# Expert selection and gate scatter of a PEER layer: two steps of one token tile, or four groups of one token tile and four heads

## The chip, the cores and the metric

The kernel runs on one core of one Trainium2 chip. The time is the device time of one execution in microseconds (us), and the figure compared is the median over runs. Engines are called PE (TensorE matmul), PEld (its weight loads), DVE (VectorE), ACT (ScalarE), POOL (GpSimd) and SP (SyncE, which issues the plain DMAs).

## What is computed

Two transformer blocks in float32 on 256 tokens of width 2048. The first is a hybrid mixer with a gated FFN, the second a mixer of two attention branches followed by a PEER layer. The change touches only the PEER layer (`peer_ffn` of the reference, here for one block of 128 tokens):

```python
q = einsum('td,dhk->thk', xb, w_q).reshape(128, 8, 2, 64)        # 8 heads, two halves
s = einsum('thpc,hpnc->thpn', q, sub_keys)                       # 128 keys per half
s1, i1 = top_k(s[:, :, 0], 16);  s2, i2 = top_k(s[:, :, 1], 16)
cand_s = s1[..., :, None] + s2[..., None, :]                     # 256 candidates per head
cand_i = i1[..., :, None] * 128 + i2[..., None, :]
top_s, pos = top_k(cand_s, 16);  expert = take_along_axis(cand_i, pos)
g = softmax(top_s)
a = gelu(einsum('thkd,td->thk', u_emb[expert], xb))
out = einsum('thk,thkd->td', g * a, v_emb[expert])
```

There are 16384 experts. Then the residual and a last RMS norm follow.

## The kernel before

**Dense experts.** The kernel gathers no rows of the two expert tables. It computes gelu(U x) for all 16384 experts, multiplies by a gate matrix that is zero where an expert was not chosen, and multiplies by V. The gate matrix is `table` in HBM (16384 experts x 256 tokens, float32), zeroed long before (32 DMAs from SP that landed in the first block's FFN). GpSimd fills it: `put(q, head)` (line 2649) issues 16 indirect DMAs of 128 elements each, which add the softmax weights `wts[q]` of one token tile q (128 tokens) and one head at the places `eidx[q]`. Each of these is one "put" below, so there are 2 x 8 x 16 = 256. The adds of different heads of one tile may hit the same element, so `put` first waits until all puts of that tile's earlier heads have landed (`g.wait_ge(d_put[q], 16 * 16 * head)`).

**Chunks and slots.** All weights stream through the core in chunks of up to 128 x 1024 float32 (512 KB), in the order `PLAN`. SP loads chunk i into one of four buffers `raw` once DVE has finished with chunk i - 4. A float32 product is made of three fp32r products of high and low parts: ACT copies the high part into one of three buffers `wh` (`cut`, line 2168), DVE subtracts it to get the low part `wl` (`cut`, line 1424), and PE runs three matmuls per 128 x 128 tile (lines 918 to 920). ACT may write `wh` of chunk i when PE is through with chunk i - 3. A slot is one chunk counted from the first U chunk, U0. U takes slots 0 to 255 (two chunks per tile of 128 experts, 24 matmuls of 256 columns each), V with its first 1024 columns takes slots 256 to 383 (12 matmuls of 512 columns each), V with its other columns comes last. In slot i, ACT and DVE cut chunk i + 2, so a cut has some two slots before PE needs it.

**High parts in PSUM.** From slot 46 to the start of V (`in_psum`, line 209), ACT makes a second copy of the high part in a PSUM buffer `ph` (line 2180; two buffers, the older must have been read), and DVE subtracts that one in place of `wh`.

**Selection.** In a written-out order, `_sides3` (line 87) hands each step of the selection to a slot. Each step has an estimated cost on DVE, a slot takes off 1.5 us of what is owed, and not more than 2.7 us may be owed. For each tile q: `top` for 8 heads (the 16 best of 128 in each half, two parts), `cand` for 4 pairs of heads (sums and the 16 best of 256, two parts), `soft` (softmax: the exponential runs on ACT between two parts of DVE), `place` (the two index halves are picked out of 16 by comparing with an iota, multiplying head by head and summing; three parts for each half) and `index` (the place in `table`, released to GpSimd by `idx_ok`). DVE works them off in its slot loop, after `read_u` (line 2094; every second slot, reads one U tile out of PSUM) and before the slot's cut. By this order tile 0 has its index in slot 48 and tile 1 in slot 96. GpSimd then issues five heads of tile 0; after the second index three times a head of tile 1 and one of tile 0; and then five heads of tile 1.

**Into V.** SP waits (line 885) until all 256 puts have landed before it loads the first gate tile `gt` (128 x 256 of `table`), and behind that load in its queue stand the V chunks. `times_gate` (DVE, line 2101) multiplies gelu by the gate two slots before PE needs the tile, `coef_high` and `coef_low` split the product. `cand` waits (`d_spill`) for a DMA that saves the tokens `x2t`, whose place it takes.

Of the kernel before, what the change touches and what calls it, by code (L numbers as in the profile page):

```python
# [12 lines left out]
ALU = mybir.AluOpType  # L13
# [72 lines left out]

def _sides3():
    at = [[] for _ in range(3 * 128 + 8)]
    work = []
    for q in range(2):  # L90
        for i in range(8):
            work += [("top", (q, i, 0), 1.95), ("top", (q, i, 1), 1.35)]
        for i in range(4):
            work += [("cand", (q, i, 0), 3.5), ("cand", (q, i, 1), 1.9)]
        work += [("soft", (q, 0), 0.3), ("soft", (q, 1), 0.9)]
        for i in range(2):
            work += [("place", (q, i, 0), 2.6), ("place", (q, i, 1), 2.3), ("place", (q, i, 2), 2.2)]
        work += [("index", q, 0.4)]
# [5 lines left out]
    for name, a, us in work:  # L104
# [5 lines left out]
        if name == "soft" and a[1] == 1 and slot == last["soft"]:  # L110
# [99 lines left out]

def in_psum(i):

    return U0 + 46 <= i < AT["V", 0, 0]
# [264 lines left out]
def build(nc, A, out):  # L478
# [179 lines left out]
    gsum = carve(8)  # L658

# [761 lines left out]
    def _(v):  # L1421
# [598 lines left out]
        def cand_3(q, i, part):  # L2020
# [5 lines left out]
            if i == 0:  # L2026
                v.wait_ge(d_spill, 16)
                v.tensor_copy(f16[:, q, :, :], x16[:, q, :, :]).then_inc(own.up(), 1)
# [6 lines left out]
        def soft_3(q, part):  # L2035
            gw = sel[:, 2, :].rearrange("p (h s) -> p h s", h=8)
            if part == 0:
                after(own.n)
                v.tensor_tensor(gw, tv[:, q, :, :], tv[:, q, :, 0:1].to_broadcast([128, 8, 16]),
                                ALU.subtract).then_inc(soft_v, 1)  # L2040
                return
            v.wait_ge(soft_a, q + 1)
            v.tensor_reduce(gsum, gw, AX.X, ALU.add).then_inc(own.up(), 1)
            after(own.n)
            v.reciprocal(gsum, gsum).then_inc(own.up(), 1)
            after(own.n)
            v.tensor_tensor(wts[q].rearrange("p (h s) -> p h s", h=8), gw, gsum.unsqueeze(2).to_broadcast([128, 8, 16]),
                            ALU.mult).then_inc(own.up(), 1)

        def place_3(q, i, part):  # L2050

            xs = f16[:, q, :, :].rearrange("p (h two) k -> p h two k", two=2)[:, :, i, :]
            after(own.n)
            if part == 0:
                if i == 0:
                    pv = tp[:, q, :, :].rearrange("p h s -> p (h s)")
                    v.tensor_scalar(tpi[:, 0, :], pv, 4, None, ALU.logical_shift_right).then_inc(own.up(), 1)
                    v.tensor_scalar(tpi[:, 1, :], pv, 15, None, ALU.bitwise_and).then_inc(own.up(), 1)
                    for n in range(2):
                        after(own.n - 1)  # L2060
                        v.tensor_copy(kf[:, n, :], tpi[:, n, :]).then_inc(own.up(), 1)
# [724 lines left out]
```

## Time and profile before

| | us |
|---|---|
| runs | 3227.93, 3237.88, 3237.24 |
| median | 3237.24 |
| the profiled execution | 3235.74 |
| its span, first to last instruction | 3233.9 |
| PE busy in it | 3190.6 (99%) |
| DVE busy | 2095.7 (65%) |
| ACT busy | 1778.7 (55%) |
| POOL busy | 458.2 (14%) |
| mean granted TensorE clock | 0.995 |

The profile is of one execution. Times in it are counted from the start of its span. The part concerned lies between 1780 us, where U begins, and 2510 us, where V has begun. Busy time of PE includes waiting inside the pipeline and overlaps, so a wait of PE is read from the view of waits and not from the share. "Issue" as what ended an idle time means that nothing which the profile shows released the engine.

### The profile page before, as it was taken

The page shows a single profiled execution, that of the slowest core. Times are in us where ns is not written, and L with a number is a line of the kernel's source. Part 1 is how long each engine was busy: PE and PEld are TensorE (multiplying, and loading weights), DVE is VectorE, ACT ScalarE, POOL GpSimd, SP SyncE. Part 2 cuts the span into 40 slices and gives each one's busy share as a digit, 9 for nine tenths or more (in the row PEclk, how much of TensorE's full clock was granted, in tenths as well). Part 3 has the DMA queues.
Part 4 walks back from the last instruction along what each step waited for, and adds up shares of the span by engine and source line. Part 5 has one row for each costly group of instructions (what it writes and reads, how often), then busy time and mean ns, then how long its engine had stood idle before and what let it go on. Part 6 is the DMA issues. An engine that isn't in the chain of part 4 may idle for free.

```text
span 3233.9 us, 58767 instructions
## 1 busy us (share of the span) xinstructions
PE 3190.6 (99%) x24234; PEld 3030.5 (94%) x24234; DVE 2095.7 (65%) x3347; ACT 1778.7 (55%) x2546; POOL 458.2 (14%) x320
## 2 busy tenths in 40 slices
PE   9999999999999999999999999999996999999998
PEld 9999999999999999999999999999996888888887
DVE  7987486666664487665665898655553666665655
ACT  5556454444444455544554468777774444444544
POOL 0000200000000100000000026677666000000000
PEclk9999999999999999999999999999998999999999
DMA  6443556666666656444555567777775777766554
GB/s 219 153 145 140 177 195 231 230 226 224 222 189 198 193 168 209 145 158 169 191 195 201 197 191 188 196 195 194 194 194 128 239 234 234 236 220 208 188 188 163
DMA packets 228698, 627.77 MB, mean 194 GB/s; under 512 B 59248, under 2 KB 77776, under 8 KB 228304
## 3 DMA queue, kind: packets, MB, share of 16 engines
q1 hardware_dynamic: 191568, 623.87, 57.8%
q0 software_dynamic: 36864, 0.15, 3.2%
q8 instruction: 192, 3.15, 0.4%
q14 instruction: 74, 0.61, 0.1%
HBM read 601.27 MB, written 21.10 MB: 192 GB/s over the span
## 4 chain that ended last, share of the span: by engine, by line
PE 79%; POOL 12%; issue 5%; DMA 2%; DVE 1%; ACT 1%; SPq 0%; POOLq 0%; DVEq 0%; ACTq 0%
PE ps L919 25%; PE ps L918 25%; PE ps L920 25%; POOL table L2654 12%; DMA table<-w_loose 1%; PE ps L973 0%; DVE wl L1430 0%; PE ps L925 0%; PE ps L945 0%; PE ps L1168 0%; DMA raw<-in_in1k 0%; ACT wh L2175 0%; PE ps L1191 0%; PE ps L1188 0%; PE ps L1360 0%
## 5 line engine op out<-in xcount | busy, mean ns | idle before, releaser
L2175 ACT CAST wh<-raw 128x1024 fp32r<-128x1024 f32 (+2 forms) x1118 | 1161.3, 1039 | 1111.5 <-PE ps L920 1077.0
L1430 DVE TENSOR_TENSOR wl<-raw,wh 128x1024 fp32r<-128x1024 f32 (+2 forms) x908 | 1092.0, 1203 | 431.2 <-ACT wh L2175 428.7
L918 PE MATMUL ps<-xh,wh 128*128 128x256 f32 x3088 | 856.1, 277 | 2.1 <-DVE wl L1430 1.3
L920 PE MATMUL ps<-xh,wl 128*128 128x256 f32 x3088 | 850.7, 275 | 0.0
L919 PE MATMUL ps<-xl,wh 128*128 128x256 f32 x3088 | 850.4, 275 | 0.0
L918 PE MATMUL ps<-xw,wh 128*128 128x258 f32 (+2 forms) x2096 | 592.6, 283 | 1.4 <-DVE wl L1430 1.3
L920 PE MATMUL ps<-xw,wl 128*128 128x258 f32 (+2 forms) x2096 | 587.7, 280 | 0.0
L918 PEld LDWEIGHTS ps<-xh,wh 128*128 128x128 f32 x3088 | 580.0, 188 | 5.3 <-issue 1.9
L919 PEld LDWEIGHTS ps<-xl,wh 128*128 128x128 f32 x3088 | 580.0, 188 | 0.1
L920 PEld LDWEIGHTS ps<-xh,wl 128*128 128x128 f32 x3088 | 579.7, 188 | 0.0
L2654 POOL DMA_INDIRECT table<-w_loose x256 | 398.2, 1556 | 948.9 <-DVE w_loose L2080 766.7
L918 PE MATMUL ps<-wh,coefs 128*128 128x512 f32 x1020 | 402.6, 395 | 28.6 <-issue 28.6
L919 PE MATMUL ps<-wl,coefs 128*128 128x512 f32 x1020 | 405.9, 398 | 0.0
L919 PE MATMUL ps<-xw,wh 128*128 128x258 f32 (+2 forms) x1441 | 404.3, 281 | 0.0
L920 PE MATMUL ps<-wh,coefs 128*128 128x512 f32 x1020 | 403.4, 395 | 0.0
L1430 DVE TENSOR_TENSOR wl<-raw,ph 128x1024 fp32r<-128x1024 f32 x210 | 255.8, 1219 | 223.2 <-ACT ph L2180 222.8
L918 PEld LDWEIGHTS ps<-xw,wh 128*128 128x128 f32 x2096 | 394.3, 188 | 4.3 <-DVE wl L1430 1.9
L920 PEld LDWEIGHTS ps<-xw,wl 128*128 128x128 f32 x2096 | 394.0, 188 | 0.0
L919 PEld LDWEIGHTS ps<-xw,wh 128*128 128x128 f32 x1441 | 270.8, 188 | 0.2
L918 PEld LDWEIGHTS ps<-wh,coefs 128*128 128x128 f32 x1020 | 196.2, 192 | 77.0 <-issue 28.8
L920 PEld LDWEIGHTS ps<-wh,coefs 128*128 128x128 f32 x1020 | 191.0, 187 | 46.1
L2108 DVE TENSOR_TENSOR coefs<-G,coefs 128x256 fp32r<-128x256 f32 x255 | 108.2, 424 | 192.0 <-ACT coefs L2544 191.7
(377 smaller groups left out, 4549.0 us busy)
## 6 DMA issues: line engine op xcount, KB each, us to landing
raw<-in_peer_u SPq DMA_DIRECT2D x256, 512.0 KB, 4.6
raw<-in_peer_v SPq DMA_DIRECT2D x256, 512.0 KB, 4.5
raw<-in_w_in SPq DMA_DIRECT2D x172, 512.0 KB, 3.6
raw<-in_w_up SPq DMA_DIRECT2D x82, 512.0 KB, 4.8
raw<-in_w_gate SPq DMA_DIRECT2D x80, 512.0 KB, 4.6
raw<-in_w_down SPq DMA_DIRECT2D x80, 512.0 KB, 4.1
raw<-in_w_out SPq DMA_DIRECT2D x64, 512.0 KB, 3.7
table<-tmp SPq DMA_DIRECT2D x32, 512.0 KB, 6.1
```

Of the source, the lines that this page charges most:

```text
L918: t.matmul(o, lh, rh, start=start, stop=False)
L919: t.matmul(o, lh, rl, start=False, stop=False)
L920: return t.matmul(o, ll, rh, start=False, stop=stop)
L1430: v.tensor_tensor(part_at(wl, i), raw[:, i % RN, 0:cols(i)], high.bitcast(F32), ALU.subtract).then_inc(lo, 1)
L2108: v.tensor_tensor(coef_at(1, n), G[:, n % 128, :], coef_at(0, n).bitcast(F32), ALU.subtract).then_inc(c_l, 1)
L2175: last = s.copy(part_at(wh, i), raw[:, i % RN, 0:cols(i)])
L2654: g.indirect_dma_start(out=table, out_offset=bass.IndirectOffsetOnAxis(ap=eidx[q][:, n:n + 1], axis=0), in_=wts[q][:, n:n + 1], in_offset= ...
```

## The change

The selection is made in four groups of one tile q and one half f of the heads (`GROUPS`: tile 0 heads 0 to 3, tile 1 heads 0 to 3, tile 0 heads 4 to 7, tile 1 heads 4 to 7), each with its own `soft`, `place` and `index`. These steps now work on 64 columns in place of 128, with costs written for that. The high parts go to PSUM from the slot of the first group's index on (`FIRST_INDEX`). GpSimd takes a head of each tile in turn after the first two, and waits for the index of a group before its first head. By the same rule of costs the four `index` steps fall in slots 25, 49, 73 and 97. The first `cand` falls in slot 12 (slot 21 before), the later ones of tile 0's first group in 16, then 36, 40, 60, 64, 84 and 88 for the other groups, all of them slots with a `read_u`; before, they were in 21, 25, 29, 33 and 69, 73, 77, 81, which have none. The three `soft` steps after the first one begin in slots 42, 66 and 90 (35 and 83 before), and `place` takes consecutive slots (20 to 24, 44 to 48, and so on) where it took every second one.

```diff
@@ -84,18 +84,21 @@
 ROOM, BEHIND = 1.5, 2.7
+GROUPS = [(0, 0), (1, 0), (0, 1), (1, 1)]
+
+
 def _sides3():
     at = [[] for _ in range(3 * 128 + 8)]
     work = []
-    for q in range(2):
-        for i in range(8):
+    for q, f in GROUPS:
+        for i in range(4 * f, 4 * f + 4):
             work += [("top", (q, i, 0), 1.95), ("top", (q, i, 1), 1.35)]
-        for i in range(4):
+        for i in range(2 * f, 2 * f + 2):
             work += [("cand", (q, i, 0), 3.5), ("cand", (q, i, 1), 1.9)]
-        work += [("soft", (q, 0), 0.3), ("soft", (q, 1), 0.9)]
+        work += [("soft", (q, f, 0), 0.25), ("soft", (q, f, 1), 0.7)]
         for i in range(2):
-            work += [("place", (q, i, 0), 2.6), ("place", (q, i, 1), 2.3), ("place", (q, i, 2), 2.2)]
-        work += [("index", q, 0.4)]
+            work += [("place", (q, f, i, 0), 2.0 - 0.6 * i), ("place", (q, f, i, 1), 1.2), ("place", (q, f, i, 2), 1.2)]
+        work += [("index", (q, f), 0.4)]
     at[0].append(("sim", 0))
     at[1].append(("sim_copy", 0))
     at[2].append(("sim", 1))
@@ -107,7 +110,7 @@
         while behind + us > BEHIND and behind > 0:
             slot += 1
             behind = max(0.0, behind - ROOM)
-        if name == "soft" and a[1] == 1 and slot == last["soft"]:
+        if name == "soft" and a[2] == 1 and slot == last["soft"]:
             slot += 1
             behind = max(0.0, behind - ROOM)
         at[slot].append((name, a))
@@ -208,9 +211,12 @@
+FIRST_INDEX = [n for n, steps in enumerate(SIDES3) if ("index", (0, 0)) in steps][0]
+
+
 def in_psum(i):
-    return U0 + 46 <= i < AT["V", 0, 0]
+    return U0 + FIRST_INDEX <= i < AT["V", 0, 0]
 def read_slot(m):
@@ -656,6 +662,9 @@
     kf = carve(256, "p (q n) -> p q n", q=2)
     sel = carve(384, "p (q n) -> p q n", q=3)
     gsum = carve(8)
+
+    def in_heads(x):
+        return x.rearrange("p (h s) -> p h s", h=8)
     fin = flatG[:, 0:2 * D].rearrange("p (q d) -> p q d", q=2)
     gain = flatG[:, 2 * D:3 * D]
@@ -2023,61 +2032,64 @@
                 top16_end(("cand", q, i), rows)
                 return
             after(own.n)
-            if i == 0:
+            if i % 2 == 0:
                 v.wait_ge(d_spill, 16)
-                v.tensor_copy(f16[:, q, :, :], x16[:, q, :, :]).then_inc(own.up(), 1)
+                v.tensor_copy(f16[:, q, 4 * i:4 * i + 8, :], x16[:, q, 4 * i:4 * i + 8, :]).then_inc(own.up(), 1)
             for h in (2 * i, 2 * i + 1):
                 va = v16[:, q, 2 * h, :].unsqueeze(2).to_broadcast([128, 16, 16])
                 vb = v16[:, q, 2 * h + 1, :].unsqueeze(1).to_broadcast([128, 16, 16])
                 v.tensor_tensor(cand[:, h, :].rearrange("p (a b) -> p a b", a=16), va, vb, ALU.add).then_inc(own.up(), 1)
             top16_begin(("cand", q, i), rows)
-        def soft_3(q, part):
-            gw = sel[:, 2, :].rearrange("p (h s) -> p h s", h=8)
+        def soft_3(q, f, part):
+            heads = slice(4 * f, 4 * f + 4)
+            gw, total = in_heads(sel[:, 2, :])[:, heads, :], gsum[:, heads]
             if part == 0:
                 after(own.n)
-                v.tensor_tensor(gw, tv[:, q, :, :], tv[:, q, :, 0:1].to_broadcast([128, 8, 16]),
+                v.tensor_tensor(gw, tv[:, q, heads, :], tv[:, q, heads, 0:1].to_broadcast([128, 4, 16]),
                                 ALU.subtract).then_inc(soft_v, 1)
                 return
-            v.wait_ge(soft_a, q + 1)
-            v.tensor_reduce(gsum, gw, AX.X, ALU.add).then_inc(own.up(), 1)
+            v.wait_ge(soft_a, GROUPS.index((q, f)) + 1)
+            v.tensor_reduce(total, gw, AX.X, ALU.add).then_inc(own.up(), 1)
             after(own.n)
-            v.reciprocal(gsum, gsum).then_inc(own.up(), 1)
+            v.reciprocal(total, total).then_inc(own.up(), 1)
             after(own.n)
-            v.tensor_tensor(wts[q].rearrange("p (h s) -> p h s", h=8), gw, gsum.unsqueeze(2).to_broadcast([128, 8, 16]),
+            v.tensor_tensor(in_heads(wts[q])[:, heads, :], gw, total.unsqueeze(2).to_broadcast([128, 4, 16]),
                             ALU.mult).then_inc(own.up(), 1)
-        def place_3(q, i, part):
-
-            xs = f16[:, q, :, :].rearrange("p (h two) k -> p h two k", two=2)[:, :, i, :]
+        def place_3(q, f, i, part):
+
+            heads, n = slice(4 * f, 4 * f + 4), slice(64 * f, 64 * f + 64)
+            xs = f16[:, q, 8 * f:8 * f + 8, :].rearrange("p (h two) k -> p h two k", two=2)[:, :, i, :]
             after(own.n)
             if part == 0:
                 if i == 0:
-                    pv = tp[:, q, :, :].rearrange("p h s -> p (h s)")
-                    v.tensor_scalar(tpi[:, 0, :], pv, 4, None, ALU.logical_shift_right).then_inc(own.up(), 1)
-                    v.tensor_scalar(tpi[:, 1, :], pv, 15, None, ALU.bitwise_and).then_inc(own.up(), 1)
-                    for n in range(2):
+                    pv = tp[:, q, heads, :].rearrange("p h s -> p (h s)")
+                    v.tensor_scalar(tpi[:, 0, n], pv, 4, None, ALU.logical_shift_right).then_inc(own.up(), 1)
+                    v.tensor_scalar(tpi[:, 1, n], pv, 15, None, ALU.bitwise_and).then_inc(own.up(), 1)
+                    for b in range(2):
                         after(own.n - 1)
-                        v.tensor_copy(kf[:, n, :], tpi[:, n, :]).then_inc(own.up(), 1)
+                        v.tensor_copy(kf[:, b, n], tpi[:, b, n]).then_inc(own.up(), 1)
                     v.wait_ge(d_iota, 16)
                     after(own.n)
-                v.tensor_tensor(eq, kf[:, i, :].unsqueeze(2).to_broadcast([128, 128, 16]),
-                                iota[:, 0:16].unsqueeze(1).to_broadcast([128, 128, 16]), ALU.is_equal).then_inc(own.up(), 1)
+                v.tensor_tensor(eq[:, n, :], kf[:, i, n].unsqueeze(2).to_broadcast([128, 64, 16]),
+                                iota[:, 0:16].unsqueeze(1).to_broadcast([128, 64, 16]), ALU.is_equal).then_inc(own.up(), 1)
             elif part == 1:
-                for h in range(8):
-                    ev = eq[:, 16 * h:16 * h + 16, :]
+                for h in range(4):
+                    ev = eq[:, 64 * f + 16 * h:64 * f + 16 * h + 16, :]
                     v.tensor_tensor(ev, ev, xs[:, h, :].unsqueeze(1).to_broadcast([128, 16, 16]),
                                     ALU.mult).then_inc(own.up(), 1)
             else:
-                v.tensor_reduce(sel[:, i, :], eq, AX.X, ALU.add).then_inc(place_ok, 1)
-                v.wait_ge(place_ok, 2 * q + i + 1)
-
-        def index_3(q):
-
+                v.tensor_reduce(sel[:, i, n], eq[:, n, :], AX.X, ALU.add).then_inc(place_ok, 1)
+                v.wait_ge(place_ok, 2 * GROUPS.index((q, f)) + i + 1)
+
+        def index_3(q, f):
+
+            n = slice(64 * f, 64 * f + 64)
             after(own.n)
-            v.scalar_tensor_tensor(sel[:, 1, :], sel[:, 0, :], 128.0, sel[:, 1, :], ALU.mult, ALU.add).then_inc(own.up(), 1)
+            v.scalar_tensor_tensor(sel[:, 1, n], sel[:, 0, n], 128.0, sel[:, 1, n], ALU.mult, ALU.add).then_inc(own.up(), 1)
             after(own.n)
-            v.tensor_scalar(eidx[q], sel[:, 1, :], float(S), iota[:, 16 + q:17 + q], ALU.mult, ALU.add).then_inc(idx_ok, 1)
+            v.tensor_scalar(eidx[q][:, n], sel[:, 1, n], float(S), iota[:, 16 + q:17 + q], ALU.mult, ALU.add).then_inc(idx_ok, 1)
         def side_3(name, a):
             if name == "top":
@@ -2089,7 +2101,7 @@
             elif name == "place":
                 place_3(*a)
             elif name == "index":
-                index_3(a)
+                index_3(*a)
         def read_u(j):
@@ -2174,7 +2186,7 @@
                 s.wait_ge(gemm, i - SN + 1)
             last = s.copy(part_at(wh, i), raw[:, i % RN, 0:cols(i)])
             if in_psum(i):
-                if i == U0 + 46:
+                if i == U0 + FIRST_INDEX:
                     s.wait_ge(sim_a, 8)
                 s.wait_ge(lo, i - 1)
                 last = s.copy(ph[:, 2 + i % 2, :], raw[:, i % RN, 0:cols(i)])
@@ -2524,9 +2536,9 @@
                         s.wait_ge(sim, 4 * a + 2 * g + p + 1)
                         s.copy(sv[:, p, 4 * g:4 * g + 4, :],
                                ps[4 + 2 * g + p][:].rearrange("p (a b) -> p a b", a=4)).then_inc(sim_a, 1)
-            elif name == "soft" and a[1] == 0:
-                gw = sel[:, 2, :].rearrange("p (h s) -> p h s", h=8)
-                s.wait_ge(soft_v, a[0] + 1)
+            elif name == "soft" and a[2] == 0:
+                gw = sel[:, 2, 64 * a[1]:64 * a[1] + 64]
+                s.wait_ge(soft_v, GROUPS.index(a[0:2]) + 1)
                 s.activation(gw, gw, ACT.Exp).then_inc(soft_a, 1)
         def activation(j):
@@ -2656,14 +2668,23 @@
         g.wait_ge(d_zero, 16 * NZERO)
         g.wait_ge(idx_ok, 1)
-        for head in range(5):
-            put(0, head)
+        put(0, 0)
+        put(0, 1)
         g.wait_ge(idx_ok, 2)
-        for head in range(3):
+        for head in range(2):
             put(1, head)
-            put(0, 5 + head)
-        for head in range(3, 8):
+            put(0, 2 + head)
+        put(1, 2)
+        g.wait_ge(idx_ok, 3)
+        put(0, 4)
+        put(1, 3)
+        put(0, 5)
+        g.wait_ge(idx_ok, 4)
+        for head in range(4, 6):
             put(1, head)
+            put(0, 2 + head)
+        put(1, 6)
+        put(1, 7)
     px.close()
     top.close()
```

## Rows read from the trace of the kernel before

**Rows 1.** Waits of PE over the whole span: total, times, longest, in us.
```profile
PE ps L918 <- issue: 28.6, 1, 28.6
PE ps L918 <- DVE wl L1430: 2.8, 4, 1.3
```

**Rows 2.** Timeline of PE, end of U and start of V.
```profile
2477.99 0.28 PE L920 MATMUL ps<-xh,wl 128*128 128x256 f32 x1
2506.88 0.76 PE L918 MATMUL ps<-wh,coefs 128*128 128x512 f32 x1 [28.62 <-issue]
...
2509.87 0.40 PE L919 MATMUL ps<-wl,coefs 128*128 128x512 f32 x1
...
2511.74 0.39 PE L918 MATMUL ps<-wh,coefs 128*128 128x512 f32 x1
```

**Rows 3.** Stretches: PE, PEld, DVE, ACT, POOL busy us (count), clock, DMA share, GB/s.
```profile
1983.00:2049.00 66.00, 64.68 (x570) 64.52 (x570) 59.12 (x109) 53.44 (x63) 42.79 (x27) 1.00 0.73 185
...
2505.00:2509.00 4.00, 2.12 (x5) 1.76 (x6) 2.23 (x4) 2.83 (x5) 0.00 (x0) 0.50 0.95 363
```

**Rows 4.** Waits of SP's queue: total, times, longest, in us.
```profile
SPq L885 <- DMA table<-w_loose: 34.5, 1, 34.5
```

**Rows 5.** Timeline of SP: the first gate load.
```profile
2497.41 0.33 SPq L888 DMA_DIRECT2D tmp<-table  x1
```

**Rows 6.** All puts: duration ns min/median/max, first and last start.
```profile
L2654 POOL DMA_INDIRECT table<-w_loose x256: 1546/1546/2392, 1915.5 to 2494.4; - x128
```

**Rows 7.** DMA issues of the page: median us from issue to landing.
```profile
table<-w_loose POOLq DMA_INDIRECT x256, 4.8
spill<-G SPq DMA_DIRECT2D x1, 2048.0 KB, 8.7
```

**Rows 8.** Puts in 1952.6:2070.3, in 2136:2339.1, in 2345.3:2465.
```profile
L2654 POOL DMA_INDIRECT table<-w_loose x48 | 76.2, 1587 | 42.9 <-issue 30.6 <-DMA table<-w_loose 12.3
L2654 POOL DMA_INDIRECT table<-w_loose x96 | 148.6, 1548 | 53.9 <-issue 53.9
L2654 POOL DMA_INDIRECT table<-w_loose x48 | 74.3, 1548 | 46.7 <-issue 34.4 <-DMA table<-w_loose 12.4
```

**Rows 9.** Timeline of DVE and POOL: the two index steps, the first put.
```profile
1914.39 0.29 DVE L2080 TENSOR_SCALAR w_loose<-G,w_loose 128x128 uint32<-128x128 f32 x1
1915.53 1.68 POOL L2654 DMA_INDIRECT table<-w_loose  x1 [766.65 <-DVE w_loose L2080]
...
2046.54 0.29 DVE L2080 TENSOR_SCALAR w_loose<-G,w_loose 128x128 uint32<-128x128 f32 x1
```

**Rows 10.** Groups of DVE in 1780:2060 by form: count, busy, mean ns.
```profile
L2069 DVE TENSOR_TENSOR G<-G 128x256 f32<-128x256 f32 x32 | 11.0, 416 | 0.0
L2064 DVE TENSOR_TENSOR G<-G,w_loose 128x2048 f32<-128x2048 f32 x4 | 9.1, 2287 | 0.2
L2072 DVE TENSOR_REDUCE G<-G 128x128 f32<-128x2048 f32 x4 | 9.1, 2276 | 0.0
L2028 DVE CAST G<-G 128x256 f32<-128x256 uint32 x2 | 0.6, 286 | 0.0
```

**Rows 11.** Timelines of ACT, DVE, PE round tile 1's softmax (slots 83 to 88).
```profile
2008.19 1.28 ACT L2530 ACT_TABLE_LOAD   x1
...
2011.66 1.28 ACT L2534 ACT_TABLE_LOAD   x1
...
2017.46 2.29 DVE L2064 TENSOR_TENSOR G<-G,w_loose 128x2048 f32<-128x2048 f32 x1
2019.67 2.34 DVE L1430 TENSOR_TENSOR wl<-raw,ph 128x1024 fp32r<-128x1024 f32 x2
...
2021.03 0.35 PE L918 MATMUL ps<-xh,wh 128*128 128x256 f32 x1 [1.32 <-DVE wl L1430]
```

**Rows 12.** Timeline of DVE: slot 25 of tile 0, a first `cand` step.
```profile
1847.95 0.75 DVE L2032 TENSOR_TENSOR G<-G 128x256 f32<-128x256 f32 x2
...
1850.97 1.21 DVE L1430 TENSOR_TENSOR wl<-raw,wh 128x1024 fp32r<-128x1024 f32 x1
```

## The prediction

> **What bounds the kernel now.** I read the waits of PE first. In 3234 us PE loses 28.6 us in one piece, and it waits for a low part four times, 2.8 us together [rows 1]. The timeline of PE puts the piece between the last U matmul (start 2477.99) and the first of V (2506.88) [rows 2]. The profile calls it "issue", so I looked for its cause on the other queues. SP waits 34.5 us for puts at line 885 [rows 4] and then issues the first gate tile at 2497.41 [rows 5], so it stood ready at 2497.4 - 34.5 = 2462.9. The last put starts at 2494.4 [rows 6]. From that gate load to the first V matmul the chain (load, gate multiply, split, cut of V chunk 0 whose load is queued behind it) takes 2506.88 - 2497.41 = 9.5 us. Everywhere else PE is full, so GpSimd counts for the time at this one place only, and an earlier end of the puts can give back no more than this piece.
>
> The stop costs a little more than its length. After it the granted clock is 0.50 of full speed, the 1.2 GHz level [rows 3]. The first seven matmul starts of V take 2509.87 - 2506.88 = 2.99 us; eight later ones take 1.87 us, 0.234 each [rows 2], so seven cost 1.64 and 1.35 us go to the slow clock. Without the stop V would start one matmul of U, 0.11 us, after 2477.99. **Removable: 2506.88 - 2478.10 + 1.35 = 30.1 us.**
>
> **Term 1: GpSimd starts earlier.** The index steps of before, slots 48 and 96, come at 1914.4 and 2046.5 [rows 9]; less the one wait of 1.3 us of PE between them [rows 1] that is 2.73 us a slot (PE's 24 matmuls, 0.114 each). The first index moves from slot 48 to 25, 23 x 2.73 = 62.8 us earlier, so the first put moves from 1915.5 [rows 9] to about 1852.7. The others fall at about 1918, 1984 and 2049.
>
> **Term 2: heads in turn.** Puts of one tile alone, 48 at a time: 76.2 + 42.9 = 119.1 us (2.48 each) beside the selection, 74.3 + 46.7 = 121.0 us (2.52 each) after it. With heads in turn: 148.6 + 53.9 = 202.5 us for 96, 2.11 each [rows 8]. The difference is mostly the landing wait before each head, some 4.1 us, three in each stretch of 48; the median put takes 4.8 us to land [rows 7]. In turn, the other tile's 16 puts cover it. Gaps called "issue" remain there (53.9 us in 96 puts); I leave them in. Before, eight heads show the landing wait; after, only head 1 of tile 0 and head 7 of tile 1 follow a head of their own tile. The first two heads end near 1852.7 + 32 x 2.11 + 4.1 = 1924, after the second index (1918); the third is wanted near 1924 + 5 x 34 = 2094 (there at 1984), the fourth near 2195 (there at 2049). So no index holds GpSimd. Sum: 1852.7 + 256 x 2.11 + 2 x 4.1 = **2401**, landed at 2406, **57 us before** SP asks for it at 2463. Heads in turn beside a selection are not in this trace. Lower bound of a put 1.85 us (1.55 busy and 0.30 between, no gap at all), which changes nothing, as the cover is there; upper bound the single rate, 2.52, nearest in kind but with waits that the new order takes out. I take 2.11. The point from which it matters is (2463 - 4.8 - 1852.7) / 256 = 2.37 us a put. Even without term 2, the old mean pace of (2496 - 1915.5) / 256 = 2.27 ends at 2433, and with it alone, started at 1915.5, the puts end at 2464, some 6 us late. The two terms are thus worth 30 us together and not apart.
>
> **Term 3: the U to V changeover without its pause.** SP gets to the gate load when it may, at 2463 or so; 9.5 us later, 2472.4, V could start, 5.7 us before U ends. I take 0. If the stop had covered work that is still due (gate tiles 1 to 3, four V chunks in one burst), it would be up to one chunk, 2.8 us. Below nothing is excluded, as U doesn't get shorter.
>
> **Term 4: DVE and ACT in U.** Nothing covers this one if it goes over the slot's budget. A cut is 1.17 us (two in 2.34) [rows 11], `read_u` (of the size of one multiply, 11.0 / 32 = 0.34 [rows 10]) comes in every second slot, so 1.39 us of a slot's 2.73 are free on average. `place`: compare and reduce over 2048 columns take 2.29 and 2.28 us [rows 10]; halves some 1.15 each. The multiplies stay one per head, so four are 1.38. The shifts, casts, `soft` and `index` on 64 columns save little, and all come four times for two. Busy DVE time grows by about 5 us over the whole selection; spread out, that is hidden, DVE being at 59 of 66 us there [rows 3]. What matters is bunching, at two places:
> - Before, tile 1's softmax made ACT load two tables (1.28 us each), DVE got its high part late, a first `place` step (compare 2.29 us) came on top, and PE waited 1.32 us at 2021.03 [rows 11]. This happens in PSUM mode, where ACT makes two copies; tile 0's softmax, outside it, cost no wait. After the change three of four groups are in PSUM mode. The first `place` step is only 1.8 us and comes a slot sooner, while DVE still waits for ACT, which helps; but five consecutive slots then carry 1.8 + 1.4 + 1.15 + 1.15 + 2.5 = 8.0 us against 5 x 1.39 = 6.95, and three `read_u` instead of 2.5. The lag is some 1.2 us, less about 0.6 of lead. I take 0.5 us of PE waiting for each group, 1.5 in all (bounds 0 and 3 x 1.5).
> - `cand` part 0 is 3.02 us [rows 12], and stands now in slots with a `read_u` (+0.34), every second one with half the copy of the indices (0.29 whole [rows 10], +0.2). In PSUM mode that makes the cut end about when PE needs it. I take 0.3 us for each of three and nothing for the other three: 1.0 (bounds 0 and 6 x 0.5).
>
> The old wait of 1.3 goes. **Term 4: +1.5 + 1.0 - 1.3 = +1.2 us**, bounds -1.3 and +6.2. The second ACT copy in slots 25 to 45 is within ACT's room (53 of 66 us busy in that mode [rows 3]): nothing. `cand` starts in slot 12 and not 21, about 1914.4 - 36 x 2.73 = 1816; the DMA that saves the tokens takes 8.7 us [rows 7] and stands in SP's queue ahead of chunk U0 + 6, reached before slot 0 (1783): it lands by 1792, some 24 us early.
>
> **Sum.** -30.1 + 1.2 = -28.9 us. The profiled execution took 3235.74 us (span 3233.9), which gives 3206.8; it is 1.5 us under the median, to which the same difference applies: **3237.2 - 28.9 = 3208.3 us**. A rate of puts up to 2.37 us leaves this as it is. From no change a measurement of this kernel can tell about 0.3%, 9.7 us.
>
> **A page against it.** The puts beside the old selection took 1.587 us on average and without it 1.548, and the whole pace was 2.48 against 2.52 [rows 8]: no loss. The Trainium skill, SBUF — State Buffer, section "Who interferes with whom", says that DVE copies, casts and tensor_scalar operations in a two-port mode keep GpSimd from the shared port pair, and with it from writing descriptors. By that rule three of four groups, with their casts and shifts, would now slow the puts.
>
> **Rivals.**
> - **GpSimd held off by the selection.** At full price every DVE side step in slots 26 to 97 stops it: the kernel's own costs are 134.2 us in the new order, three quarters are 101 us, so the puts end at 2502 and not 2401, landed 2507, 10 us later than before: 3247 us. With only copies, casts and shifts counted (some 20 of at most 0.3 us) it is 6 us, and the forecast stands. Against it are [rows 8]. 3%: 2 within 0.3%, 1 slower. The lock is the one of the Trainium skill's page SBUF — State Buffer, named above.
> - **The turn doesn't pay**: heads in turn beside the selection run at 2.52. The puts end at 1852.7 + 645 = 2498: no gain, 3237; between 2.37 and 2.52 a part (at 2.44, 3224). For it: the "issue" gaps aren't understood. Against: 96 puts in a row at 2.11. 4%, half of that within 0.3%.
> - **The slower case: cuts come late in U.** In slots 25 to 97 DVE or ACT, not PE, sets the pace. To end over 0.3% slower they must add 30 + 10 = 40 us in 72 slots, 0.55 us a slot; DVE would be busy over 2.73 us a slot where it has 59 of 66. At 0.6 a slot: 3237 - 30 + 43 = 3250 us. One wait of 1.3 in the same mode speaks against. 3%.
> - **A new stop at the changeover** (gate tiles or splits late): 5 to 20 us of the 30 stay, 3213 to 3228. 3%, mostly still faster.
> - **The change does not do what it says** (an index later than its slot): 1%.
>
> The forecast has 86%. Faster by over 0.3% (under 3227.5) 0.90 (86, 2 of the turn, 2 of the changeover), within 0.3% 0.06 (2 + 2 + 1 + 1), slower 0.04 (3 + 1). Range: term 4 gives 3206 to 3215; terms 3 and the runs' own spread (3227.9 to 3237.9, so a median may sit 5 or 6 us off) widen it, and the partial cases above: **3200 to 3222**.
>
> **What would show it.** PE's wait called "issue" at the end of U gone, SP's wait on line 885 gone, last put near 2400, first near 1853, about two landing waits of POOL, clock 1.00 through the changeover; PE's waits for low parts in U between 1 and 6 us, near the last three softmaxes. Wrong if: the puts end after 2463; PE waits for DVE over 8 us in U; V starts with a new wait; or the time gained in U and V doesn't show at the end.

## The result, and the profile after

The changed kernel takes **3186.97 us** (median of four runs, 3186.34 to 3187.43) against 3235.23 (four runs, 3227.93 to 3237.88): ratio 0.986, 95% interval 0.983 to 0.989. It is faster by 48 us where 29 were forecast, and lies below the range. The profiled execution went from 3235.74 to 3187.06 us, its span from 3233.9 to 3185.3, so 48.6 us are to be found in the trace.

The waits of PE over the whole span (total, times, longest, in us) no longer have the stop of [rows 1]; the first line is now that of the late low parts.

```profile
PE ps L927 <- DVE wl L1439: 2.4, 5, 0.8
```

The timeline of PE where U meets V answers to [rows 2]: V's first matmul starts 0.12 us after U's last, 27.1 us earlier than before.

```profile
2479.57 0.28 PE L928 MATMUL ps<-xl,wh 128*128 128x256 f32 x1
2479.68 0.28 PE L929 MATMUL ps<-xh,wl 128*128 128x256 f32 x1
2479.80 0.40 PE L927 MATMUL ps<-wh,coefs 128*128 128x512 f32 x1
2480.03 0.39 PE L928 MATMUL ps<-wl,coefs 128*128 128x512 f32 x1
```

All puts, the puts of heads in turn (window 1924:2365; busy and idle us), and the first gate load of SP, which answer to [rows 6], [rows 8] and [rows 5]:

```profile
L2666 POOL DMA_INDIRECT table<-w_loose x256: 1546/1547/2287, 1852.1 to 2402.7; - x128
```
```profile
L2666 POOL DMA_INDIRECT table<-w_loose x210 | 326.0, 1552 | 115.6 <-issue 115.6
```
```profile
2464.69 0.37 SPq L897 DMA_DIRECT2D tmp<-table  x1
```

GpSimd starts at 1852.1 (forecast 1852.7), makes a put in (326.0 + 115.6) / 210 = 2.10 us (2.11), and is done at 2404 (2401), 60 us before SP asks. So this half went as forecast. From V's first matmul to the end of the span, though, it is 3185.3 - 2479.8 = 705.5 us, against 3233.9 - 2506.9 = 727.0 before: **21.5 us are gained inside V**, which the change doesn't touch. The views of stretches show where. In 2700 to 2900 us, in the middle of V, with PE full and the clock at 1.00 in both, the kernel before and then the changed one (columns as in [rows 3]):

```profile
2700.00:2900.00 200.00, 200.00 (x858) 161.93 (x858) 132.26 (x201) 96.45 (x143) 0.00 (x0) 1.00 0.69 229
```
```profile
2700.00:2900.00 200.00, 200.00 (x884) 165.62 (x883) 132.38 (x193) 100.11 (x148) 0.00 (x0) 1.00 0.71 235
```

The count in brackets takes in the one or two matmuls under way at the start of the stretch. From start to start, averaged over stretches of 30 us, a 512-column matmul takes 0.2333 us before and 0.2267 us after, throughout V (but for the few at the low clock and the end). 3072 of them (256 tiles of 12) make 20.5 us. With 1.35 us for the low clock after the stop that makes 21.8, close to the 21.5. In U both kernels have 0.1133 us for 256 columns.

### The profile page after: what moved, and what is told of

It reads as the page before. It is cut to its first block, busy times and chain, and to the rows that moved or that the text cites. A ratio compares the mean times of both kernels' runs of the same rounds, so it can differ in the third digit from the quotient of the medians.

```text
span 3185.3 us, 58834 instructions
## 1 busy us (share of the span) xinstructions
PE 3170.9 (100%) x24234; PEld 3027.4 (95%) x24234; DVE 2099.0 (66%) x3377; ACT 1803.4 (57%) x2573; POOL 458.2 (14%) x320
## 4 chain that ended last, share of the span: by engine, by line
PE 96%; DVE 2%; ACT 1%; issue 0%; DMA 0%; POOL 0%; SPq 0%; DVEq 0%; ACTq 0%; POOLq 0%
PE ps L927 31%; PE ps L928 31%; PE ps L929 31%; DVE wl L1439 1%; PE ps L982 0%; ACT wh L2187 0%; PE ps L934 0%; PE ps L954 0%; DVE G L2080 0%; DVE G L2083 0%; DVE G L2075 0%; PE ps L1177 0%; DMA raw<-in_in1k 0%; PE ps L1200 0%; PE ps L1197 0%
## 5 line engine op out<-in xcount | busy, mean ns | idle before, releaser
L1439 DVE TENSOR_TENSOR wl<-raw,wh 128x1024 fp32r<-128x1024 f32 (+1 forms) x887 | 1066.7, 1203 | 425.5 <-ACT wh L2187 422.9
L1439 DVE TENSOR_TENSOR wl<-raw,ph 128x1024 fp32r<-128x1024 f32 x231 | 281.0, 1219 | 226.7 <-ACT ph L2192 226.3
L929 PE MATMUL ps<-wh,coefs 128*128 128x512 f32 x1020 | 396.8, 389 | 0.0
L927 PE MATMUL ps<-wh,coefs 128*128 128x512 f32 x1020 | 396.8, 389 | 0.0
L928 PE MATMUL ps<-wl,coefs 128*128 128x512 f32 x1020 | 396.8, 389 | 0.0
L2192 ACT CAST ph<-raw 128x1024 fp32r<-128x1024 f32 x231 | 232.6, 1007 | 0.0
```

The lines of the kernel that those rows point to most:

```text
L927: t.matmul(o, lh, rh, start=start, stop=False)
L928: t.matmul(o, lh, rl, start=False, stop=False)
L929: return t.matmul(o, ll, rh, start=False, stop=stop)
L1439: v.tensor_tensor(part_at(wl, i), raw[:, i % RN, 0:cols(i)], high.bitcast(F32), ALU.subtract).then_inc(lo, 1)
L2192: last = s.copy(ph[:, 2 + i % 2, :], raw[:, i % RN, 0:cols(i)])
```

## The experiments

What was open: does this spacing belong to the stop, to the program, or to chance? All times are medians, ratios are to the kernel before in the same call. "Slow" and "fast" below are the spacings 0.2333 and 0.2267 of V's matmuls.

**1. Before, without the stop.** `e1_before_fewer_puts` leaves out the puts of two heads of tile 1, so its gate table lacks these heads:

```diff
-        for head in range(3, 8):
+        for head in range(3, 6):
             put(1, head)
...
-                    y.wait_ge(d_put[1], 16 * 128)
+                    y.wait_ge(d_put[1], 16 * 96)
```

> The kernel before, with the puts of heads 6 and 7 of tile 1 left out (the gate table lacks these two heads), and SP waiting for the other 96 of that tile. The last two heads took 82 + 31 us with their waits, so the puts land before 2463 us, when SP asks, and V follows U without a stop. Nothing else differs from before: same selection, same DVE and ACT order. Theory S (the stop of PE ahead of V also sets the spacing of V's matmuls for all that follows: 0.2333 us after a stop, 0.2267 without): spacing 0.2267 us, time 3235 - 30 - 20.5 = 3185 us. Rival P (the spacing belongs to the program, by where its code and buffers lie, and the change altered that): spacing stays 0.2333, time 3205 us. Rival R (it comes and goes by chance from run to run): either, and runs that spread by 20 us.

3185.55 us (3184.89 to 3185.76), ratio 0.984 (0.983 to 0.986); the stop gone, spacing fast:

```profile
2700.00:2900.00 200.00, 200.00 (x884) 165.62 (x883) 132.59 (x192) 99.37 (x148) 0.00 (x0) 1.00 0.73 236
```

The whole gain comes with the old selection and the old order of the slots, so without the stop V runs fast. The changed program as a cause of its own falls.

**2. The change with the stop put back.** Two kernels of one edit each hold GpSimd back until the third index (long) or the second (short).

```diff
-        g.wait_ge(idx_ok, 1)
+        g.wait_ge(idx_ok, 3)        # e3_after_hold_short: 2
         put(0, 0)
```

> The changed kernel, with GpSimd made to wait for the third index (slot 73, about 1984 us) before its first put. Same work. The puts end about 132 us later, at 2534, land at 2539, and V's first matmul comes 9.5 us later, near 2548, against 2480: a stop of some 69 us, and the clock at half speed for 1.35 us. Theory S: the spacing of V's matmuls goes to 0.2333, so 3187 + 69 + 1.3 + 20.5 = 3278 us. Rival P: spacing stays 0.2267, 3257 us.

3268.72 us (3243.04 to 3272.67). The profile is of the longest: a stop of 62.8 us, the spacing slow. The run at 3243.04 has no trace; it lies 22 to 30 us under the others, about what the fast spacing would make of it.

```profile
2700.00:2900.00 200.00, 200.00 (x859) 161.96 (x858) 134.73 (x214) 96.88 (x144) 0.00 (x0) 1.00 0.72 232
```

> The changed kernel, with GpSimd made to wait for the second index (slot 49, about 1918 us) before its first put: heads in turn, but no earlier start than before the change. The puts end near 2404 + 66 = 2470, land at 2475, V starts 9.5 us later at 2484.5 and not at 2479.8: a stop of about 5 us. My sum for this case in the prediction: such a kernel's puts come some 6 us late. Theory S: even the short stop sets the spacing to 0.2333: 3187 + 5 + 20.5 = 3212 us. If it takes a stop long enough for the clock to fall, spacing 0.2267 and 3192 us. Rival P: 3192 us.

Runs at 3187.76, 3193.81, 3208.95 and 3213.23 us. The profile is of the second: a stop of 4.4 us, the spacing fast afterwards.

```profile
2479.20 0.28 PE L929 MATMUL ps<-xh,wl 128*128 128x256 f32 x1
2483.88 0.77 PE L927 MATMUL ps<-wh,coefs 128*128 128x512 f32 x1 [4.40 <-issue]
```

The low clock (0.43 us a matmul) lasted for 12 matmuls here, longer than after the stop of 28.6 us, and V ran fast all the same. So the low clock doesn't bring the slow spacing, and a stop brings it in some runs only. The runs near 3209 and 3213 fit the slow spacing (+20.5 us); they have no trace.

**3. Early start alone.** `e4_after_no_turns`: the four groups, but heads one after the other within each.

```diff
+        for n, (q, f) in enumerate(GROUPS):
+            g.wait_ge(idx_ok, n + 1)
+            for head in range(4 * f, 4 * f + 4):
+                put(q, head)
```

> The changed kernel with the four groups and their early start, but GpSimd takes the four heads of each group one after the other: twelve landing waits of 4.1 us are exposed in place of two. Puts at 2.5 us each less the three changes of tile: 1852 + 256 x 2.5 - 12 = 2480, landed 2485, V starts at 2494 and not 2480: a stop of 10 to 18 us. Theory S: 3187 + 14 + 20.5 = 3222 us with spacing 0.2333 (1.3 more if the clock falls). Rival P: 3201 us.

Runs at 3186.47, 3189.29, 3207.15 and 3207.76 us. The profile (of the first) shows 12 landing waits of 3.9 us, the last put at 2461.6, and a wait of 1.8 us of SP:

```profile
POOL table L2666 <- DMA table<-w_loose: 46.7, 12, 4.9
```
```profile
SPq L894 <- DMA table<-w_loose: 1.8, 1, 1.8
```

A put took (2463.2 - 1851.6) / 256 = 2.39 us and not 2.5, so no stop is left where one of 14 was expected: V's first matmul starts 0.12 us after U's last. The early start alone takes the stop away, with little to spare (in part 2 a wait of 9.9 us of SP made a stop of 4.4, so some 5.5 us of such a wait cost nothing). The turns buy the 60 us of margin. Two of the four runs lie 20 us over the other two, as the slow spacing would make them. Whether these two had a short stop isn't known, as neither was traced.

**4. Stops inside V.** `e5_after_mid_stops`: PE waits at tile 64 of each half of V for a chain of six small DMAs.

```diff
+    held = alloc(top, "held", [128, 4])
...
+            if j == 64:
+                t.wait_ge(d_hold, 16 * 6 * (half + 1))
             taken(AT["V", j, half])
```

> The changed kernel with two stops put into V: PE waits at tile 64 of each half of V for six small DMAs of GpSimd in a chain, which begin when tile 62 is done. Each chain takes 12 to 26 us, less 2.7 us for tile 63: two stops of 10 to 22 us, 20 to 44 us together. Theory S1 (a stop of PE in a stream of 512-column matmuls decides the spacing anew, mostly to 0.2333 us): spacing 0.2267 up to the first stop, 0.2333 after it in most runs, up to 2304 x 0.0067 = 15 us more, and the runs differ by amounts that fit one or both stretches. Rival S3 (only the changeover from U to V decides it, the stop there matters because V begins after it): 0.2267 throughout, 3187 + stops + 3 us for the clock, and runs within 2 us of each other.

3256.20 us (3255.86 to 3258.57). Two stops, 29.1 us together. Stretches of V ahead of the first, between the two, and after the second:

```profile
2560.00:2660.00 100.00, 100.00 (x443) 82.80 (x442) 70.16 (x111) 49.49 (x74) 0.00 (x0) 1.00 0.75 243
2720.00:2920.00 200.00, 200.00 (x859) 161.97 (x858) 130.96 (x196) 96.61 (x144) 0.00 (x0) 1.00 0.71 229
3090.00:3235.00 145.00, 145.00 (x623) 117.44 (x622) 85.74 (x104) 70.12 (x104) 0.00 (x0) 1.00 0.56 188
```

(623 - 1) / 145 is 4.29 a us, as (859 - 2) / 200; the first stretch has (443 - 1) / 100 = 4.42. In the traced run one stop in mid-stream turned fast into slow, and the second did not turn it back. It isn't a matter of the changeover alone.

Stops and spacing don't make up the whole time. V begins at 2501.28 here and at 2479.80 in the changed kernel, 21.5 us later, though nothing is put in ahead of it. The edit also allocates a buffer of 16 bytes in a partition (`held`) ahead of the buffers of the first block. In the down projection of its FFN, the changed kernel and then this one:

```profile
920.00:1120.00 200.00, 200.00 (x1767) 200.00 (x1766) 100.30 (x94) 88.37 (x108) 18.01 (x13) 1.00 0.64 195
920.00:1120.00 200.00, 200.00 (x1687) 200.00 (x1687) 96.51 (x90) 84.73 (x105) 18.07 (x12) 1.00 0.63 186
```

That is 0.1133 us for a 256-column matmul against 0.1186 on average. The stage loses 11.3 of the 21.5 us; most of the others go at 1555 to 1750 us, at 0.118 us a matmul. In program order the new buffer moves the moving operand there (`a`) by 16 bytes and leaves the stationary one (`wh`) where it was. U, whose operands are all allocated ahead of `held`, kept its 0.1133. No run tests this cause by itself.

**5. Is it the idle PE?** `e6_long_hold_busy` fills the long stop with 640 matmuls on the ones tile (128 x 128 ones in plain float32, each recorded as two, the result unused); `e10_after_ones_between` puts 12 of them between U and V of the changed kernel, where nothing is late; `e7_before_run_up` puts 40 behind the stop of the kernel before.

```diff
             if n == 0:
                 t.wait_ge(sim_a, 8)
+                t.wait_ge(ev_u, 125)
+                keep_busy(ps[0][:, 0:128], 12)     # e7: 40; e6: 640, ahead of the waits
```

> The changed kernel with GpSimd held until the third index, as in the run with the long stop (62.8 us, spacing 0.2333, 3268.7 us), but PE fills the stop with 640 matmuls of 128 x 128 on the ones tile ahead of V, about 0.113 us each, 72 us: V starts without a pause, near 2552 us. Theory S1 (it is the idle PE): spacing 0.2267 in every run, 3187 + 72 = 3259 us, runs within 2 us. Rival S4 (it is what the late gate brings: V's chunks and gate tiles come in a burst after it, and V runs in another relation to its cuts and loads): spacing 0.2333, 3280 us.

3348.66 us (3348.41 to 3349.47): they took 142.9 us, 0.223 each and not 0.113, hence the time; PE never idle, clock 1.00, V's data long there when it began, and V slow. So the slow spacing needs neither an idle PE nor data that come late for V's first matmul.

> The kernel before with its stop of 28.6 us as it is, and 40 matmuls of 128 x 128 on the ones tile after the wait of V's first tile, ahead of V's first matmul. They take 5 to 8 us, partly at the low clock, of which V would lose 1.35 anyway. Theory S2 (the low clock under V's first matmuls decides the spacing): V begins at full clock and runs at 0.2267: 3236.7 + 5 - 20.5 = 3221 us. Theory S1 in the form that the pause itself decides it, whatever comes first after it: spacing 0.2333 in most runs, 3242 us. If the run-up refills what the pause emptied, S1 too gives 0.2267: then this run can't tell S1 from S2, but it is a repair that costs 5 us and gives 20.

Ten runs from 3221.57 to 3246.24 us, median 3238.75: no repair. The profile (of a run at 3242.81) has the slow spacing; four runs under 3229 fit the fast one.

> The changed kernel, no stop, with 12 matmuls on the ones tile (float32, 0.214 us each as measured, 2.6 us) between U's last and V's first matmul, V's operands being there in time. Theory S5: what comes between breaks the take-over although PE is never idle and the clock full: spacing 0.2333 in most or all runs, 3187 + 2.6 + 20.5 = 3210 us. Rival S1 in its first form (it needs an idle PE): 0.2267, 3189.6 us; the long stop filled with such matmuls ran at 0.2333, which speaks against it, but there V's data also came late. Rival S6 (late data): 3189.6 us.

3208.93 us, six runs within 3208.05 to 3209.83. No stop, no low clock, nothing late, and slow:

```profile
2478.77 0.28 PE L929 MATMUL ps<-xh,wl 128*128 128x256 f32 x1
2478.89 2.84 PE L934 MATMUL ps<-ones 128*128 128x128 f32 x24
2481.49 0.48 PE L927 MATMUL ps<-wh,coefs 128*128 128x512 f32 x1
```
```profile
2700.00:2900.00 200.00, 200.00 (x859) 161.99 (x858) 129.66 (x192) 97.11 (x144) 0.00 (x0) 1.00 0.72 229
```

**6. Matmuls of U's kind behind the stop.** `e9_before_u_like_run_up`, the result thrown away:

```diff
+                for k in range(16):
+                    three(ps[0][:, 0:S], row_at(wh, AT["V", 0, 0], k % 8), row_at(wl, AT["V", 0, 0], k % 8), *x4(k), True, True)
```

> The kernel before with its stop, and after the wait of V's first tile 48 matmuls of U's kind (fp32r, 256 columns of the normed tokens against V's first chunk, into a PSUM bank that is free; their result is thrown away) ahead of V's own. They cost 5.4 us at full clock; the low clock falls on them. Theory S5 (V takes over the regular spacing of the stream ahead of it if that is U's kind and nothing comes between; after a stop or other matmuls the spacing is decided anew, mostly to the slow one): 0.2267 in every run, 3236 - 20.5 + 5.4 = 3221 us, runs within 3 us. Rival S6 (the spacing is redrawn at V's start whatever the stream ahead was, if V's data came late): 0.2333 in most runs, 3241 us, runs 20 us apart as with the run-up on the ones tile.

3220.89 us, ten runs within 3218.29 to 3223.91, ratio 0.996 (0.994 to 0.999), spacing fast in the profile. The kernel before had 5 of 21 runs of the same call at 3214 to 3219 and the others at 3232 to 3243. So what stands directly ahead of V's first matmul matters: U's kind brings the fast spacing even after a stop, and the ones matmuls of part 5 don't.

**7. Another shape.** `e8_before_half_columns`: each 512-column matmul of V as two of 256.

> The kernel before with each 512-column matmul of V made as two of 256 columns (twice the matmuls and weight loads, the same products; the stop stays). U's 256-column matmuls have run at 0.1133 us in every trace so far, twice that is 0.2267. If the slow spacing is a matter of 512-column matmuls alone, V runs at 0.1133 after the stop as well: 3236.7 - 20.5 = 3216 us. If a stop slows any shape, 256 columns take 0.1167 or 0.120: 3237 to 3257 us.

3235.98 us (3228.16 to 3247.89): no gain. Its V matmuls took 0.1183 us, twice that is 0.237, where U's take 0.1133 at the same width. So halving the columns doesn't bring 0.2267; it brings a third value, some 10 us longer over V than the slow spacing. The time stays equal because the stop of the traced run was 17.9 us and not 28.6 (its puts landed earlier, and SP waited 23.7 us and not 34.5). Width alone doesn't set the spacing. This pointed to V's operands, which part 8 tests.

**8. Where the operands lie.** V's stationary operands (the tiles that PEld loads) are the coefficients, two halves in one buffer at columns 4 and 580. Five kernels move them (a column is 4 bytes), one of them (e13) with the 12 ones matmuls of part 5. The edit of e11, e12 and e13:

```diff
-    ch, cl = [coefs[:, o:o + 2 * S].rearrange("p (n t) -> p n t", t=S) for o in (4, 580)]
+    ch, cl = [coefs[:, o:o + 2 * S].rearrange("p (n t) -> p n t", t=S) for o in (0, 512)]
```

> The kernel before with the two halves of the coefficients, V's stationary operands, at columns 0 and 512 of their buffer and not at 4 and 580. Same work. If the slow spacing comes from where V's operands lie against each other in SBUF, it changes with this: another value than 0.2333 after the stop, 3072 times the difference in the time (0.2267: 3215 us; 0.240: 3256 us). If it has nothing to do with places: 0.2333 in most runs, 3236 us.

> The changed kernel with the same move of the coefficients (columns 0 and 512). Without a stop. If the places decide only how a broken spacing settles, V still takes over U's: 0.2267, 3187 us. If they are part of why the take-over works, another spacing and another time, by 3072 times the difference.

> The changed kernel with the 12 matmuls on the ones tile between U and V (3208.9 us, 0.2333, in all six runs) and the coefficients moved to columns 0 and 512. If what comes ahead of V only matters with the old places of the coefficients: 0.2267 in every run, 3186 + 2.6 = 3189 us. If the move helped only after an idle PE: 0.2333, 3209 us.

> The kernel before, stop and all, with only the low half of the coefficients moved, from column 580 to 516: the high half stays at 4, the two are 512 columns apart, as in the kernel with both at 0 and 512. If the distance of the halves decides: 0.2267 in every run, 3216 us. If the start decides: 0.2333 in some three of four runs, 3235 us, with a few runs near 3216.

> The kernel before with both halves shifted by four columns, from 4 and 580 to 0 and 576: the start moves, the distance of 576 columns stays. If the start decides: 0.2267 in every run, 3216 us. If the distance decides: 0.2333 in some three of four runs, 3235 us. If neither alone does, both this kernel and the one with the low half moved are near 3235 us.

| kernel | columns | median (range), us | runs |
|---|---|---|---|
| before, same calls | 4, 580 | 3234.6 and 3235.6 (3212.1 to 3243.5), 13 of 44 under 3221 | 44 |
| e14, before | 4, 516 | 3235.37 (3217.45 to 3239.14), 4 of 12 under 3221 | 12 |
| e11, before | 0, 512 | 3216.43 (3210.23 to 3218.59) | 10 |
| e15, before | 0, 576 | 3216.24 (3212.95 to 3220.14) | 12 |
| e13, change and ones | 0, 512 | 3189.64 (3189.37 to 3190.14) | 4 |
| e12, change | 0, 512 | 3185.95 (3185.57 to 3186.29) | 4 |

The stop is still there in e11, and V is fast behind it:

```profile
2507.70 0.77 PE L918 MATMUL ps<-wh,coefs 128*128 128x512 f32 x1 [29.62 <-issue]
```
```profile
2700.00:2900.00 200.00, 200.00 (x884) 165.66 (x883) 134.78 (x205) 100.20 (x148) 0.00 (x0) 1.00 0.74 236
```

The two kernels that tell start from distance, e14 and then e15:

```profile
2700.00:2900.00 200.00, 200.00 (x858) 161.95 (x858) 132.18 (x201) 96.41 (x143) 0.00 (x0) 1.00 0.71 229
2700.00:2900.00 200.00, 200.00 (x884) 165.78 (x883) 135.58 (x205) 99.53 (x148) 0.00 (x0) 1.00 0.73 236
```

One run of each kernel was traced; the others are told apart by their times, 20 us apart. A shorter stop would also make a run shorter, but the 13 runs under 3221 us have a mean clock of 0.994 or 0.995 like most of the rest, where the run of part 7 with a stop of 17.9 us has 0.997.

The start decides, not the distance of the halves: with each half starting four columns (16 bytes) lower, no time of 26 runs with a stop or other matmuls ahead of V fits the slow spacing. With the start at column 4, 39 of the 56 runs above do, and all six behind the ones matmuls. The share changes from call to call: in the three earlier calls only 1 of 30 runs of the kernel before was under 3221. Which half's start matters wasn't tested. Ratio of e15 to before: 0.995 (0.993 to 0.997). The move alone is worth some 19 us of the kernel before and nothing of the changed one, whose V is fast already. The two together (e12) are the fastest version that computes everything, 1.0 us under the changed kernel in another call; I don't count that as a gain, but with the move the fast spacing no longer hangs on V following U without a break (e13).

## Why the prediction was wrong, and where it was right

- **What bounds the kernel**: right. PE was full but for the one stop, and the stop came from SP's wait for the last puts. Without it (part 1) the gain is there with nothing else changed.
- **Terms 1 and 2**: right in each number (start 1852.1, 2.10 us a put, two landing waits of 7.7 us together, end 2404). That the two were worth 30 us only together was off. Its own sum for the early start alone (2433) said so, and part 3 shows it, with heads in a row at 2.39 us a put over the whole and not 2.5. Turns alone (part 2, short hold) made SP wait 9.9 us where the sum had some 6 us, and left a stop of 4.4 us. The limit of 2.37 us a put left out that V could start 5.7 us before U ends (term 3); with these it is 2.39.
- **Term 3**: right at the changeover, no pause. Its last sentence was wrong: "Below nothing is excluded, as U doesn't get shorter" looked at U and left out V.
- **Term 4**: forecast +1.2 us. U's last matmul starts at 2479.68 and not 2477.99, +1.7, of which 0.1 was there when U began. PE waits three times at the three `place` stretches behind the softmaxes, one of them

```profile
1917.38 0.36 PE L927 MATMUL ps<-xh,wh 128*128 128x256 f32 x1 [0.52 <-DVE wl L1439]
```

  and slips by 0.08 us twice at each of the three `cand` steps with the index copy, about half of the 0.3 taken. The old wait of 1.3 is gone. Part 1, with the old order of the slots, is 1.4 us faster than the changed kernel.
- **The step that failed** is the price of the stop, the first term of the sum: "The stop costs a little more than its length", 30.1 us with 1.35 for the clock. I read the spacing behind the stop, 0.234 us from [rows 2], as V's own speed and compared only the seven slow matmuls with it. The stop cost 28.8 + 1.35 + 20.5 = 50.6 us, and part 1 gets it back with the stop alone. Part 8 adds that the 20.5 hang on the columns of the coefficients too: at 0 and 576 the kernel before keeps its stop and loses only the rest. With the 50.6 the sum is 3235.7 - 50.6 + 1.2 = 3186.3 against the 3187.06 of the profiled execution. A hint stood in the rows: U's 570 matmuls of 256 columns in 64.68 us of busy time [rows 3] are 0.1135 each, twice that 0.227. It was a hint only, since V's own matmuls of 256 columns take 0.1183 (part 7).
- **Rivals**: all were other ways for the stop to stay or for U to slow down, none for V to speed up. GpSimd was not held off by the selection: a put kept 1.552 us of busy time against 1.548 [rows 8], with three of four groups beside the puts. The Trainium skill, SBUF — State Buffer, section "Who interferes with whom", would have casts and shifts in a two-port mode keep the port from GpSimd; in these traces no loss can be seen.

## What to carry to other kernels

A stop of PE may cost more than its length: compare the spacing of the matmuls behind it with that of the same shape ahead of it, and take that of half the shape as a hint, before taking the one behind as given. When PE is full and the clock at 1.00, count matmul starts in equal stretches of two kernels; a difference of 3% there is invisible in busy shares and in the waits. Try the placement of the stationary operand by 16 bytes when a stream of matmuls runs slower than a like one, and judge it over ten or more runs, since one run can show either spacing. Look at stages far from the edit as well: a small buffer that an experiment adds moves what is allocated behind it (part 4).

## What the runs showed of the hardware

- One and the same stream of fp32r matmuls (512 columns, a new stationary tile each) keeps one of two spacings over hundreds of us, 0.2267 or 0.2333 us, 3% apart at the full clock. Which one it takes was settled where the stream began or went on after a break, in every trace. Directly behind U's kind of matmuls it was the fast one in all six traces (the change, e1, e4, e5 up to its first stop, e9, e12). By their times, two untraced runs of e4 near 3207 us may be exceptions, or had a short stop. Behind a stop it varies from run to run (before: 13 of 44 runs under 3221 us); behind the ones matmuls it was slow in all ten runs without a stop (e6 and e10, one traced of each).
- It depends on where the stationary operand starts: 16 bytes lower, and the slow one did not come. Why is open. No places but the four of part 8 were tried, and V's moving operands were not moved. In the down projection of e5 a 256-column stream went from 0.1133 to 0.1186 us on average when a buffer of 16 bytes ahead of its moving operand was added.
- The Trainium skill, TensorE: Matmul & The Clock Gate, section "Back-to-back issue gap", gives some 216 ns from one matmul of 512 columns to the next as the isolated gap at full clock, and about 131 ns sustained in a stream of weight loads and matmuls. Here no traced stretch of V came to either: 226.7 and 233.3 ns.
- After a stop of only 4.4 us (e3) the granted clock was 1.2 GHz for 12 matmuls (5 us), after 28.6 us (before) for seven (3 us). The length of the stop doesn't tell what the clock costs behind it.
- GpSimd's gaps of 3 to 5 us marked "issue", some 18 in the 256 puts, stay with heads in turn (115.6 us in 210 puts with the 0.30 between puts) and are still not explained.
